# A decoder step with a gathered expert layer: two mixer programs joined into one, the memory state in another buffer, and the first eight v gathers ahead of the expert stage's barrier

## The reference, cut to what matters

```python
def trunk_layer(x, c, ...):
    sh1, sc1, gt1, sh2, sc2, gt2 = split(silu(c) @ ada_w + ada_b, 6)
    h = rmsnorm(x, g_mix) * (1 + sc1) + sh1
    z = h @ w_in                      # 1024 -> 3336 columns
    hm, C1, n1, m1 = mlstm(q, k, v, ig, lf, C0, n0, m0)
    oa = swa_attend(qa, k_all, v_all, ...)          # window of 128 and the new keys
    yc = cb * short_conv(cc * ch, cbuf, conv_w)
    x = x + gt1 * (concat([hm, oa, yc]) @ w_out)
    h = rmsnorm(x, g_ffn) * (1 + sc2) + sh2
    x = x + gt2 * peer_ffn(h, wq, subkeys, u_tab, v_tab)

def block(xb):                        # peer_ffn
    q = (xb @ wq).reshape(256, 8, 2, 128)
    s = einsum('thpd,pkd->thpk', q, subkeys)
    s1, i1 = top_k(s[:, :, 0], 16);  s2, i2 = top_k(s[:, :, 1], 16)
    idx, g = the 16 best of the 256 sums s1 + s2, softmax of their scores
    act = gelu(einsum('thkd,td->thk', u_tab[idx], xb))
    return einsum('thk,thkd->td', g * act, v_tab[idx])
```

## Time and profile before

| | us |
|---|---|
| median of three timed runs | 2052.15 (2051.05 to 2056.47) |
| the profiled execution: its span, first to last instruction | 2046.0 |
| busy: PE, DVE, POOL, ACT | 1616.0, 1207.7, 1134.0, 476.3 |
| first program (prompt mixers), until DVE has passed the barrier | 509.15 |
| second program (sample mixer) | 509.15 to 714.85 |
| third program (experts), from POOL's first instruction | 714.85 to 2046.0 |
| DMA, mean over the span | 349 GB/s |

### The profile page before, as it was taken

One profiled execution on the slowest core, in us unless ns is written; L12 is line 12 of the kernel. 1 busy time (PEld: TensorE's weight loads), 2 busy tenths in 40 slices (PEclk: granted clock), 3 DMA queues, 4 the chain that ended last, 5 costly groups with the idle time before them and its releaser, 6 DMA issues.

```text
span 2046.0 us, 20838 instructions
## 1 busy us (share of the span) xinstructions
PE 1616.0 (79%) x5461; PEld 764.0 (37%) x5461; DVE 1207.7 (59%) x3129; ACT 476.3 (23%) x1217; POOL 1134.0 (55%) x1168
## 2 busy tenths in 40 slices
PE   6979989983767457768888888788878789599966
PEld 1524546451126113223433344333433344255422
DVE  2222355867766701116767766677667689679972
ACT  1221313130101021212223222222222223223321
POOL 3000021322873555777777667767777677577773
PEclk8989999996775679998999989899999899899988
DMA  8795676896995599999999999999999999799995
GB/s 319 254 364 207 215 263 218 305 337 135 355 385 179 198 401 404 392 416 394 400 420 420 400 368 418 419 373 420 420 401 391 388 403 419 308 412 417 414 372 226
DMA packets 237575, 713.43 MB, mean 349 GB/s; under 512 B 23102, under 2 KB 49056, under 8 KB 237457
## 3 DMA queue, kind: packets, MB, share of 16 engines
q0 software_dynamic: 156672, 570.49, 71.2%
q1 hardware_dynamic: 80488, 140.73, 19.4%
q10 hardware_dynamic: 312, 1.07, 0.2%
HBM read 704.42 MB, written 8.25 MB: 348 GB/s over the span
## 4 chain that ended last, share of the span: by engine, by line
PE 19%; DMA 14%; DVE 12%; issue 7%; POOL 7%; ACT 5%; DVEq 0%; POOLq 0%; ACTq 0%
PE ps_y L2316 13%; DVE u_rows L2095 6%; DMA v_rows<-in_peer_v_dram,expert_idx_ring 5%; DMA v_rows<-in_peer_v_dram,tile_idx 5%; PE ps_r L2290 4%; POOL u_rows L1890 3%; DMA u_rows<-in_peer_u_dram,expert_idx_ring 3%; POOL v_rows L1896 2%; POOL v_rows L1904 2%; ACT wt_diag L1987 2%; PE ps_y L2331 2%; DMA v_rows<-in_peer_v_dram,sample_idx 1%; DVE key_scores_w L2106 1%; ACT L2002 1%; ACT L2033 1%
## 5 line engine op out<-in xcount | busy, mean ns | idle before, releaser
L2316 PE MATMUL ps_y<-v_rows,wt_diag 128*128 128x512 f32 x1664 | 796.9, 621 | 146.6 <-DMA v_rows<-in_peer_v_dram,expert_idx_ring 65.2
L2316 PEld LDWEIGHTS ps_y<-v_rows,wt_diag 128*128 128x128 f32 x1664 | 311.4, 197 | 571.1 <-issue 547.5
L1890 POOL DMA_INDIRECT u_rows<-in_peer_u_dram,expert_idx_ring x384 | 368.2, 959 | 164.7 <-issue 90.3
L2095 DVE CUSTOM_DVE_ANT_0 u_rows<-u_rows,ps_y 128x1024 f32<-128x1024 f32 x360 | 420.4, 1218 | 64.1 <-DMA u_rows<-in_peer_u_dram,expert_idx_ring 58.1
L1896 POOL DMA_INDIRECT v_rows<-in_peer_v_dram,expert_idx_ring x384 | 366.7, 955 | 120.2 <-issue 99.3
L341 POOL DMA_INDIRECT low_rows<-in_peer_u_dram,tile_idx x128 | 174.7, 1364 | 214.7 <-DVE tile_dots L333 148.5
L607 PE MATMUL ps_z<-w_stream,hT 128*128 128x512 f32 (+5 forms) x560 | 249.0, 602 | 36.9 <-DMA w_stream<-in_w_in_dram 19.7
L2331 PE MATMUL ps_y<-v_rows,wt_diag 64*64 64x512 f32 x1024 | 135.1, 645 | 57.4 <-DMA v_rows<-in_peer_v_dram,tile_idx 50.8
L333 DVE CUSTOM_DVE_ANT_0 low_rows<-low_rows,tile_rows 128x1024 f32<-128x1024 f32 x128 | 152.9, 1232 | 44.1 <-DMA low_rows<-in_peer_u_dram,tile_idx 31.9
L607 PEld LDWEIGHTS ps_z<-w_stream,hT 128*128 128x128 f32 (+1 forms) x560 | 100.9, 185 | 163.9 <-issue 132.6
L1904 POOL DMA_INDIRECT v_rows<-in_peer_v_dram,tile_idx x128 | 122.1, 954 | 71.8 <-PE ps_y L2331 44.6
(11 more groups left out here) (434 smaller groups left out, 1628.3 us busy)
## 6 DMA issues: line engine op xcount, KB each, us to landing
w_stream<-in_w_in_dram SPq DMA_DIRECT2D x25, 2048.0 KB, 12.8
w_stream<-in_ada_w_dram SPq DMA_DIRECT2D x12, 2048.0 KB, 12.8
w_stream<-in_peer_wq_dram SPq DMA_DIRECT2D x8, 1024.0 KB, 8.5
wq<-in_peer_wq_dram SPq DMA_DIRECT2D x4, 2048.0 KB, 42.2
w_stream<-in_w_in_dram SPq DMA_DIRECT2D x5, 1568.0 KB, 8.5
w_stream<-in_w_in_dram SPq DMA_DIRECT2D x5, 1536.0 KB, 17.5
u_rows<-in_peer_u_dram,expert_idx_ring POOLq DMA_INDIRECT x384, 7.4
v_rows<-in_peer_v_dram,expert_idx_ring POOLq DMA_INDIRECT x384, 7.9
```

The source lines that it names most:

```text
L1890: g.indirect_dma_start(u_rows[:, j, :], None, U, bass.IndirectOffsetOnAxis(where[:, j:j + 1], 0))\
L2095: v.tensor_tensor_reduce(u_rows[:, j, :], u_rows[:, j, :], row[:, :], 1.0, 0.0, ALU.mult, ALU.add, dots[:, par, j:j + 1]).then_inc(s["u_us ...
L2316: mm = nc.tensor.matmul(ps_y[:, c * 512:(c + 1) * 512], diag[:, par, j, :], v_rows[:, j, c * 512:(c + 1) * 512], start=(first and j == 0), ...
```

## The change

1. `mix_prompt` and `mix_sample` become one program, `mixers`. The barrier between them is gone; each engine goes on from tile 3 to the sample rows, and explicit waits stand where the barrier stood (PE for the residual of tile 3, `x1_ready`; SP for its store, `x1_stored`; DVE for the nine stores of the prompt's states, `state_out`).
2. The tables are new. Gap (3, "Z") is gone; the pairs of head 6 move from before the residual of tile 3 to the sample gap A, the keys of head 7 to gap D, its pairs to gap E. The dots in the sample gaps are 95 (89 before), and gap M gets six.
3. The copy of hT is a function of its own (`dve_columns`) and stands ahead of gap A.
4. The order of SP's loads changes: kc waits until the eighth `pairs` is done, C goes into other buffers of `w_stream` and is issued once SVCB stands in PSUM, ahead of vc, and the two DRAM copies come last.
5. w_out lies in the buffer `v_rows`, which now lasts through both stages; so POOL can issue the first eight v gathers at the end of the mixers, once `out_product` of the sample rows is done (`first_v_rows`).
6. The exponential and the division of tile 0's gates move from the start of the experts to the end of the mixers; the first `sums0` stands ahead of the transpose of the subkeys.

```diff
-GAPS = [(t, w) for t in range(1, NT) for w in "BCDEFGHIJRA"] + [(NT - 1, "Z")] + [("sample", w) for w in "ABCDEFGKLMNOZ"]
-KEYS_IN = {..., (3, "H"): 6, (3, "Z"): 7}
-PAIRS_IN = {..., (3, "F"): 5, (3, "A"): 6, (3, "Z"): 7}
+GAPS = [(t, w) for t in range(1, NT) for w in "BCDEFGHIJRA"] + [("sample", w) for w in "ABCDEFGKLMNOZ"]
+KEYS_IN = {..., (3, "H"): 6, ("sample", "D"): 7}
+PAIRS_IN = {..., (3, "F"): 5, ("sample", "A"): 6, ("sample", "E"): 7}
-           ... (3, "R"): 4, (3, "Z"): 6,
-           ("sample", "A"): 7, ("sample", "B"): 6, ("sample", "C"): 5, ("sample", "D"): 3, ("sample", "E"): 8,
-           ("sample", "F"): 5, ("sample", "G"): 5, ("sample", "K"): 6, ("sample", "L"): 9, ("sample", "N"): 12,
-           ("sample", "O"): 12, ("sample", "Z"): 11}
+           ... (3, "R"): 4,
+           ("sample", "A"): 3, ("sample", "B"): 3, ("sample", "C"): 6, ("sample", "D"): 3, ("sample", "E"): 8,
+           ("sample", "F"): 7, ("sample", "G"): 8, ("sample", "K"): 8, ("sample", "L"): 11, ("sample", "M"): 6,
+           ("sample", "N"): 12, ("sample", "O"): 10, ("sample", "Z"): 10}
...
+    def first_v_rows(self, pool, V):
+        for j in range(NB):
+            self.nc.gpsimd.indirect_dma_start(self.keep["v_rows"][:, j, :], None, V,
+                                              bass.IndirectOffsetOnAxis(self.keep["idx0"][:, j:j + 1], 0))\
+                .then_inc(self.keep["v_first"], 16)
+
+    def act_exp(self, act):
+        act.wait_ge(self.s["a_routed"], PH)
+        self.nc.scalar.activation(self.keep["gate0"][:, :], self.keep["gate0"][:, :], ACT.Exp).then_inc(self.s["a_exp"], 1)
...
-        self.cT_out = self.hT[:, 0:4, :]
+        self.cT_out = self.dm[:, :, :]
...
+    def dve_columns(self, dve):
+        self.t_landed(dve, T_H1)
+        self.nc.vector.tensor_copy(X.hT[:, 4:8, 0:n], X.ps_t[:, :, 0:n]).then_inc(self.s["t_free"], 1)
...
-    Cs = X.wr[:, 0, :, :]...   CTs = X.wr[:, 1, :, :]...   Km = X.wr[0:NS, 2, :, :]...
+    Cs = X.wr[:, 1, :, :]...   CTs = X.wr[:, 2, :, :]...   Km = X.wr[0:NS, 0, :, :]...
...
     def sync(sp):                     # the sample rows' part of SP's program
+        sp.wait_ge(P0["x1_stored"], 16 * (1 + NT))
         sp.dma_start(X.xr[0:NS, :], I["x_sample"].rearrange("b t d -> (b t) d")).then_inc(s["xr_in"], 16)
         for i in range(RING, len(CHUNKS)):
             X.stream.load(sp, I, "sample", i)
+        sp.wait_ge(P0["a_routed"], PH)
         sp.dma_start(kc, ...)
+        sp.dma_start(stc, ...)
+        T.z_landed(sp, SVCB)
+        sp.dma_start(Cs, ...)
+        sp.dma_start(nq, ...);  sp.dma_start(n8, ...)
         sp.dma_start(vc, ...)
-        ... nq, n8, stc, the two cache copies
-        T.z_landed(sp, CCCH)
-        T.z_landed(sp, OZ)
-        sp.dma_start(Cs, ...)
...
     def gpsimd(pool):
         A.gathers(pool, U, "sample", "O")
         A.gathers(pool, U, "sample", "Z")
+        T.on(pool, "o_full")
+        A.first_v_rows(pool, I["peer_v"][0])
...
     def vector(dve):
+        T.dve_columns(dve)
         T.gap(dve, "A")
+        dve.wait_ge(P0["state_out"], 16 * (5 + MH))
         T.dve_front(dve, chain, K)
...
         T.dve_residual(dve, chain)
+        X.ahead.gates(dve, T.chain0)
         T.gap(dve, "Z")
...
     def tensor(pe):
         T.transpose_rows(pe, K)
+        pe.wait_ge(P0["x1_ready"], NT)
+        pe.wait_ge(P0["pool_done"], NT)
+        X.ahead.settled(pe, NT, 0)
         T.project(pe, K)
...
-                for i in range(GPT - 1):          # experts, POOL
+                for i in range(1, GPT - 1):
                     for j in range(NB):
                         v0_gather(i, j)
...
-                a(gate0[:, :], gate0[:, :], ACT.Exp).then_inc(s["exp0"], 1)
                 a(wts0[:, :], wts0[:, :], ACT.Gelu_apprx_tanh).then_inc(s["act0"], 1)
...
+                slot0(0)                          # experts, PE
                 pe.wait_ge(s["sub_in"], 16)
                 ... transpose of the subkeys
-                slot0(0)
```

638 lines of the change are left out of this document (320 added, 318 removed), and 2 rows, old and new, of the table DOTS_IN.

## The result

| | before | changed |
|---|---|---|
| median of seven runs, us | 2051.05 (2047.40 to 2056.51) | 2034.79 (2030.71 to 2043.63) |
| ratio | | 0.9925, 95% interval 0.9903 to 0.9947 |
| span of the profiled execution, us | 2046.0 | 2028.9 |

The change makes the kernel faster by 0.75%, 15 to 16 us. I had forecast -33 us (2019, taken off the 2052.15 of three runs) and a range of 1998 to 2040: the direction is right, the size is less than half. The rival nearest to the median is the hidden head start (2030), but as will be seen it is not what happened.

What follows compares the result with a forecast made beforehand. DMA engines bound the expert stage and the sample stage's first half, while other waits rule around the barrier. Terms -25.5 - 2.8 + 5.8 - 10.4 = -32.9 us, taken off 2052.15, give 2019; range 1998 to 2040.

Steps and rivals of the forecast that it cites:

- the hidden head start: Experts: early v gathers gain nothing because another engine later sets the end; -22.5 us in all, 2030; chance 0.13.
- The marks: Trace signs of being right, among them PE's first sample chunk near 478 and DVE's first sample dot near 484.
- the passage: From tile 3 to the sample rows, barrier removed: first sample dot at 483.7 instead of 509.15, -25.5 us.
- Step 1: Barrier and passage into the sample stage: -25.5 us, with the front half staying 101.6 us; bounds -33 and -16.
- The bound that I gave as -33: Step 1's low end: all of the front half runs at 392 GB/s, 94 us instead of 101.6.
- The other bound: Step 1's high end, -16 us: head 7's keys and pairs (3.8 and 5.5 us) lengthen the front half in full.
- Step 2: Back half to the memory update's end: PE's wait for C goes, gap M's dots come late; -2.8 us.
- Step 3: Tail of the mixers: fewer u gathers, eight v gathers that must land before the barrier; +5.8 us, bounds 0 and +13.
- Step 4: Experts: eight of 896 gathers, 4.2 MB, leave a stage whose DMA engines are full; -10.4 us, bounds 0 and -13.
- My condition: Step 4: if the ninth v gather comes within 6.5 us of the experts' start, the 10.4 us count in full.
- The starved POOL: Fuller gaps: POOL writes gather descriptors slowly beside DVE's dots; +3 to +24 us (2055 to 2076); chance 0.08.

Runs made afterwards that it cites:

- e2: Changed kernel with the last four sample weight chunks loaded only to half (sample outputs wrong); 2029.15 us, ratio 0.9902.
- e13: Changed kernel with one of eight row blocks of the last four sample weight chunks loaded (sample outputs wrong); 2035.05 us, ratio 0.9924.
- e3: Changed kernel with keys and pairs of head 7 each done twice in the sample stage; 2038.92 us, ratio 0.9921.
- e1: Changed kernel with the eight early v gathers put back into the expert stage; 2030.28 us, ratio 0.9895.
- e14: Changed kernel with no v gathers ahead and DVE's expert loop written out; 2008.37 us, ratio 0.9788.
- e10: Kernel before the change with DVE's expert loop written out; 2029.98 us, ratio 0.9896.
- e4: Changed kernel with PE taking the second group of v rows before the next rows' transposes in the experts; 2034.68 us, ratio 0.9911.
- e16: Changed kernel with DVE's expert loop written out and PE taking the second v group before the next rows' transposes; 2011.49 us, ratio 0.9805.

## Why the prediction was wrong, step by step

**The marks and the passage were right.** PE's first sample chunk at 479.09 (forecast 478.3), the first dot at 484.16 (483.7), no wait for C.

**Step 1 failed at "leave the front half as long as it was, 101.6 us".** I reckoned 1.6 MB more of gathers against 1.5 MB that leave. Nothing left: the copies and vc still move within the half, C came into it, and the gathers that had moved during the 34 us of the passage had to go somewhere. It is 4.6 MB more, 41.4 instead of 36.8. The changed kernel with few bytes has a floor (e2 101.9 us with 37.2 MB; e13 100.8 with 34.0), the kernel before took as long (101.6 with 36.8), and the bytes lifted the changed one to 109.0. The seven us are real: 101.0 and 101.6 in the two traces of the program before, 105.5 to 110.5 in the ten of the new one. The bound that I gave as -33, all of the half at 392 GB/s in 94 us, was no bound at all: e13 shows that not even 34.0 MB do it. The other bound, that head 7's keys and pairs come on top, did not happen (e3). The sum of the step, -25.0 + 7.4 = -17.6, lies near my bound of -16, for a reason that I had not named; that is luck.

**Step 2** gave -1.0 for -2.8. The wait for C is gone as said; in its place PE waits 7.65 us for a copy that stands on DVE behind the M dots (611.00), and the memory update ran for 14.00 us as before (640.49; granted clock 0.53 over the back half, where 0.50 is the lower level of 1.2 GHz). The other traces of the merged mixers have 61.2 to 64.2 us, the two of the program before 63.5 and 67.3, so -1.0 and -2.8 cannot be told apart.

**Step 3 was right**: +4.4 for +5.8. By e1 and e14 the sum has two larger parts: three u gathers fewer give 9.5 us (40.6 to 31.1), the eight v gathers cost 12 to 14, where I had reckoned 12. POOL's part in the barrier holds, as I took it to, until what it issued has landed (the stage began 8.64 us after POOL's last gather row and 3.0 after the last landing; before, the 9.41 us also held DVE's last dots).

**Step 4 gave -2.8 for "-10.4", and failed at leaving the rest of the experts as it was.** It has two terms. (a) The stage's first part became shorter by 6.8. The sign and the mechanism hold: 399 and 392 GB/s over 186.36 and 179.55 us are 74.4 and 70.4 MB, the eight gathers less. But the size is less sure than two traces make it look: e10, the same program as before up to there, took 190.48 us, and the kernels with none ahead 188.4 to 191.5. Against these the changed kernel is 9 to 12 us shorter, as forecast, so the 3.6 us that seem to be missing are within what two executions differ by. What is real is that the seventeenth gather waited for PE's transposes: e4 and e16 gain 3.8 to 4.1 us with PE's order alone. My condition looked at the ninth gather only (it came at 7.9 us), and not at what stands between the first and the second group in PE's program. (b) The rest became longer by 4.0, where I had put nothing, and that is the stall at DVE's jump, 9.23 for 4.46. The change had taken nine instructions out of DVE's program, and the loop landed elsewhere. No row of the experts in my groups would have told that; a look at the idle times put down to nothing would have shown the 4.46 us, though not that it would double. The half's 7.4 us and these 4.0 are the parts of the shortfall that the experiments show.

**The starved POOL** did not come, as I had it at 0.08. Gathers do take 1.99 us beside DVE's dots and 0.94 once these are over at 684.91 (the rows of the tail), in line with what the Trainium skill (SBUF — State Buffer, Who interferes with whom) says of contention and against what it infers for descriptor generation beside a tensor_tensor. But in the front half the DMA engines were full either way.

**The rival "head start hidden anyway"** came out at nearly the measured time, and is wrong all the same: the head start is worth 9 to 12 us in the first part of the experts. What cancels it is the tail, which it lengthens by 12 to 14 us, and beside it the stall costs some 4.7 us that have nothing to do with it. Its -22.5 would have needed the front half as long as before.

## What to carry to other kernels

When a barrier or a wait is removed, count the bytes that moved during it: they fall into the next stage, and so do those of each load that comes earlier; then ask whether that stage was at the DMA limit or at a floor of its own, since in this kernel the bytes cost time only above the floor. Work done ahead of a barrier is paid in the barrier itself when the engine that issued it must wait for it to land; compare the whole from the last common mark to the next. And when a difference of a few microseconds sits in code that was not touched, line up the n-th event of both traces before explaining it: here it was one jump.

## What the runs showed that I had not expected

- DVE stands still for 4.43 to 4.46 or for 9.05 to 9.27 us when it jumps back over its 1120 instructions, and for nothing between. Which of the two depends on how many instructions stand ahead of the loop (nine more: the short one). Behind the branch there is always a stop of 5.3 to 5.5 us; the long stall has a second one of 4.7 to 4.8 us, one or three records further on, at a fixed place of the code. Packets of the instruction queue come in both. The second stop alone cost the gathers time.
- Writing DVE's loop out is worth 21 us in the kernel before (2051.36 to 2029.98, timed together) and, by the ratios, 19 to 26 in the changed ones; that one line gives at least about as much as the whole change (ratios 0.9896 and 0.9925, whose intervals overlap).
- One and the same program gave a first sample dot at 481.4 to 487.9 us and halves of 105.5 to 110.5 us. The experts up to the ring's first gather took 186.4 and 190.5 us in two traces of the program before. A single trace tells no difference below some 5 us, unless the row itself is the same to a few hundredths, as the stall was.
